# Decoder trunk on one core: the first norm's input read with channels on partitions

## What is computed

```
y = x * rsqrt(mean(x*x over channels) + 1e-6) * gain
layer 0:  x = x + dsa_attention(norm(x)) ;  x = x + swiglu(norm(x))
layer 1:  x = x + short_conv(norm(x))    ;  x = x + swiglu(norm(x))
```

## Time and profile before

| | us |
|---|---|
| median of 3 runs | 2071.18 |
| the profiled execution | 2071.52 |
| its span | 2069.9 |
| TensorE busy in the span | 2062.3 |
| VectorE busy | 1698.5 |
| ScalarE busy | 1177.7 |

### The profile page before, as it was taken

How to read it: one execution, slowest core, us unless ns; L and a number is a source line. 1 busy time by engine, 2 the same in 40 slices (tenths; PEclk the granted TensorE clock), 3 DMA queues, 4 the chain that set the end, 5 groups by cost and what they waited for, 6 DMA issues and landing times.

```text
span 2069.9 us, 27700 instructions
## 1 busy us (share of the span) xinstructions
PE 2062.3 (100%) x9421; PEld 1712.9 (83%) x9421; DVE 1698.5 (82%) x1933; ACT 1177.7 (57%) x1487; POOL 105.7 (5%) x128
## 2 busy tenths in 40 slices
PE   9999999999999999999999999999999999999999
PEld 8888888888888888888888888888888888888887
DVE  6777668999999987867798787579999999978766
ACT  6548656556655654545555554566656565654453
POOL 0000000100010000000000000000000000000000
PEclk9999999999999999999999999999999999999999
DMA  8564456777777776767666766567777777767674
GB/s 276 166 196 150 141 166 203 231 230 224 227 223 234 217 230 199 222 201 210 205 206 203 215 200 201 175 200 221 225 231 218 234 228 229 216 219 215 199 219 147
DMA packets 226722, 432.10 MB, mean 209 GB/s; under 512 B 14432, under 2 KB 21232, under 8 KB 226640
## 3 DMA queue, kind: packets, MB, share of 16 engines
q1 hardware_dynamic: 209328, 399.23, 58.8%
q0 software_dynamic: 17168, 31.75, 8.9%
q10 hardware_dynamic: 144, 0.03, 0.0%
HBM read 428.86 MB, written 2.10 MB: 208 GB/s over the span
## 4 chain that ended last, share of the span: by engine, by line
PE 97%; DVE 2%; ACT 1%; issue 1%; ACTq 0%; DVEq 0%
PE ps L733 24%; PE ps L735 24%; PE ps L734 24%; PE ps L589 3%; PE ps L522 3%; PE ps L524 3%; PE ps L523 3%; PE ps L590 3%; PE ps L591 3%; PE ps L538 2%; PE ps L695 1%; PE ps L693 1%; PE ps L694 1%; PE ps L648 1%; DVE w_lo L1356 0%
## 5 line engine op out<-in xcount | busy, mean ns | idle before, releaser
L1356 DVE TENSOR_TENSOR w_lo<-stage,w_hi 128x1024 fp32r<-128x1024 f32 x688 | 830.3, 1221 | 224.9 <-ACT w_hi L962 221.3
L962 ACT ACTIVATE w_hi<-stage 128x1024 fp32r<-128x1024 f32 x688 | 709.8, 1054 | 490.8 <-PE ps L735 365.6
L733 PE MATMUL ps<-w_hi,xs 128*128 128x512 f32 x1122 | 439.4, 392 | 0.3
L735 PE MATMUL ps<-w_hi,xs 128*128 128x512 f32 x1122 | 437.0, 389 | 0.0
L734 PE MATMUL ps<-w_lo,xs 128*128 128x512 f32 x1122 | 436.6, 389 | 0.0
L733 PEld LDWEIGHTS ps<-w_hi,xs 128*128 128x128 f32 x1122 | 210.7, 188 | 44.2 <-DVE gated L1637 1.1
L735 PEld LDWEIGHTS ps<-w_hi,xs 128*128 128x128 f32 x1122 | 210.6, 188 | 44.1
L734 PEld LDWEIGHTS ps<-w_lo,xs 128*128 128x128 f32 x1122 | 210.7, 188 | 42.9
L733 PE MATMUL ps<-w_hi,hs 128*128 128x512 f32 x584 | 227.6, 390 | 0.0
L735 PE MATMUL ps<-w_hi,hs 128*128 128x512 f32 x584 | 227.2, 389 | 0.0
L734 PE MATMUL ps<-w_lo,hs 128*128 128x512 f32 x584 | 227.2, 389 | 0.0
(11 more groups left out here) (217 smaller groups left out, 3041.2 us busy)
## 6 DMA issues: line engine op xcount, KB each, us to landing
stage<-in_w_gate SPq DMA_DIRECT2D x176, 512.0 KB, 4.0
stage<-in_w_up SPq DMA_DIRECT2D x176, 512.0 KB, 5.0
stage<-in_w_down SPq DMA_DIRECT2D x176, 512.0 KB, 5.0
stage<-in_conv_w_in SPq DMA_DIRECT2D x96, 512.0 KB, 4.9
stage<-in_attn_w_in SPq DMA_DIRECT2D x48, 512.0 KB, 4.4
stage<-in_w_gate POOLq DMA_DIRECT2D x86, 256.0 KB, 5.7
stage<-in_attn_w_out SPq DMA_DIRECT2D x32, 512.0 KB, 4.6
stage<-in_conv_w_out SPq DMA_DIRECT2D x32, 512.0 KB, 4.3
```

What stands on the lines that cost most here:

```text
L733: pe.matmul(ps[:, bank, :], hi, b_hi, start=start, stop=False)
L735: return pe.matmul(ps[:, bank, :], lo, b_hi, start=False, stop=stop)
L962: nc.scalar.activation(w_hi[:, j % RING, :], stage[:, at, :], ACT.Copy).then_inc(hi_done, 1)
L1356: tt(w_lo[:, p, :], stage[:, stage_at(first + j), :], f32(w_hi[:, p, :]), ALU.subtract).then_inc(lo_done, 1)
```

## The change

The host hands x over a second time, as `x_turned[p, k, t]` = x[token t, channel 128 k + p]. This is loaded into the same bytes of `res`, seen as 16 channel tiles of 256 tokens (`x_cols`). ScalarE and VectorE read it there instead of PSUM, and TensorE's transposes of x go. The identity is loaded after x and the first block. The rows are loaded into `res` during block 2, four loads. The squares are taken per channel tile; VectorE adds the 16 tiles to one, and TensorE sums over partitions by two matmuls with a column of ones. The steps that follow are put one to two slots later. TensorE issues 15 matmuls on the zeroed tile in one run.

```diff
-            sp.dma_start(mat.ap(), ident).then_inc(in_ident, 16)
-            load_x(x_part(0), in_x[0])
+            load_x(0, 2, in_x[0])
             load_front(0, 0)
-            load_x(x_part(1), in_x[1])
+            load_x(2, 4, in_x[1])
             load_front(0, 1)
             for j in range(1, 4):
-                load_x(slice(WIDE * j, WIDE * (j + 1)), in_x[j + 1])
+                load_x(4 * j, 4 * j + 4, in_x[j + 1])
                 load_front(0, 2 * j)
                 load_front(0, 2 * j + 1)
+            sp.dma_start(mat.ap(), ident).then_inc(in_ident, 16)
             for b in range(1, len(FRONT)):
                 for s in range(FRONT_SLOTS):
                     load_front(b, s)
+                    if b == 2 and s % 2:
+                        load_rows(s // 2)
...
+            def load_x(k0, k1, arrived):
+                sp.dma_start(x_cols[:, k0:k1, :], x_turned[:, k0:k1, :]).then_inc(arrived, 16)
+            def load_rows(j):
+                if j == 0:
+                    sp.wait_ge(res_squared, 4)
+                    sp.wait_ge(xs_ready, 4)
+                cols = slice(WIDE * j, WIDE * (j + 1))
+                sp.dma_start(res[:, :, cols], x[:, cols].rearrange("(a p) n -> p a n", p=P)).then_inc(in_rows, 16)
...
+            def sum_columns():
+                pe.wait_ge(squares_added, 5)
+                for a in range(2):
+                    mm = pe.matmul(ps[:, X_SUM_BANK, a:a + 1], square[:, 0, a * P:(a + 1) * P], ones[:, :],
+                                   start=True, stop=True)
+                mm.then_inc(first_summed, 1)
...
-            steps = {(1, 6): [lambda: index_turn(0)], (2, 0): [lambda: score_heads(0)],
+            steps = {(1, 2): [sum_columns], (1, 7): [lambda: index_turn(0)], (2, 1): [lambda: score_heads(0)],
...
-            warm(7)
-            pe.wait_ge(in_ident, 16)
-            turn_x(0)
-            warm(3)
-            turn_x(1)
-            warm(3)
+            warm(15)
             for b in range(len(FRONT)):
                 for s in range(FRONT_SLOTS):
                     front_slot(b, s)
-                    if b == 0 and s + 2 < 8:
-                        turn_x(s + 2)
...
-                    nc.scalar.activation(xs[:, k, 0:TOK], ps[:, X_BANKS[h % 4], TOK * m:TOK * (m + 1)],
+                    nc.scalar.activation(xs[:, k, 0:TOK], x_cols[:, k, :],
                                          ACT.Copy, scale=gain[:, 0, k:k + 1]).then_inc(res_hi, 1)
...
+            def x_square(j):
+                nc.scalar.activation(x_squares[j][:, :, :], x_cols[:, 4 * j:4 * j + 4, :],
+                                     ACT.Square).then_inc(res_squared, 1)
...
+            steps = {(1, 0): [lambda: x_square(0)], (1, 1): [lambda: x_square(1)],
+                     (1, 2): [lambda: x_square(2)], (1, 3): [lambda: x_square(3)],
+                     (1, 6): [first_root_step, lambda: evict(0), head_weights],
+                     (2, 3): [lambda: index_copy(0), lambda: evict(1)], (2, 5): [lambda: relu(0)],
...
+            def first_sum_a():
+                add_squares(square[:, :, :], cross[:, :, :], 0, 2)
+            def first_sum_b():
+                add_squares(sums[:, :, :], gated[:, :, :], 0, 4)
+            def first_sum_c():
+                add_squares(square[:, :, :], sums[:, :, :], 2, 4)
+                add_squares(square[:, 0:2, :], square[:, 2:4, :], 3, 4)
+                add_squares(square[:, 0, :], square[:, 1, :], 4, 4)
...
+            steps = {(1, 0): [set_score], (1, 2): [first_sum_a], (1, 3): [first_sum_b], (1, 4): [first_sum_c],
+                     (1, 6): [first_scale, lambda: rotate(0)],
+                     (2, 1): [head_tables], (2, 3): [lambda: rotate(1)], (2, 5): [lambda: add_scores(0)],
```

More of the change, by code:

```diff
@@ L80, in landed, with trunk @@
     return 16 * (n // DEEP + 1) + 16 * (loop_slots // DEEP) * i
-def trunk(nc, x, attn_w_in, attn_w_out, conv_w_in, conv_w_out, w_gate, w_up, w_down,
+def trunk(nc, x, x_turned, attn_w_in, attn_w_out, conv_w_in, conv_w_out, w_gate, w_up, w_down,
           gains, head_gains, conv_taps, tables_h, tables_i, ident, bounds, out):
@@ L127, in trunk @@
         rs = sb("rs", [P, 4, 2])
-        sb("to_64_bytes", [P, 10])
+        ones = sb("ones", [P, 1])
+        sb("to_64_bytes", [P, 9])
         part = ExitStack()
@@ L192, in trunk @@
         warm_rows = pt[:, 0:P]
+        x_cols = res[:, :, :].rearrange("p a (k t) -> p (a k) t", t=TOK)
+        x_squares = (square, cross, sums, gated)
         swapped, roped, squared = (by_rows(buf) for buf in (cross, sums, square))
@@ L233, in trunk @@
         rs_ready = sem("rs_ready")
-        x_turned = sem("x_turned")
+        in_rows = sem("in_rows")
+        squares_added = sem("squares_added")
         x_low = sem("x_low")
@@ L324, in merged @@
             return out
-        X_BANKS = (2, 3, 6, 7)
+        X_SUM_BANK = 4
         FRONT_BANKS = ((0, 1), (2, 3))
@@ L331, in trunk @@
         INDEX_HEADS = tuple(tuple(12 + h if i == 0 else 4 * (i - 1) + h for h in range(4)) for i in range(4))
-        def x_part(h):
-            return slice(2 * P * h, 2 * P * (h + 1))
         def x_low_done(engine, h):
@@ L432, in load_block @@
                     load(n + s, s % DEEP, w[s * 2 * P:(s + 1) * 2 * P, base:][:, bass.ds(col, width)], width)
-            def load_x(cols, arrived):
-                sp.dma_start(res[:, :, cols], x[:, cols].rearrange("(a p) n -> p a n", p=P)).then_inc(arrived, 16)
+            def load_x(k0, k1, arrived):
[6 more added lines that the diff above has]
+                sp.dma_start(res[:, :, cols], x[:, cols].rearrange("(a p) n -> p a n", p=P)).then_inc(in_rows, 16)
             def load_front(b, s):
@@ L529, in stream_rows @@
                         other()
-            pe.wait_ge(warm_set, 1)
+            pe.wait_ge(warm_set, 2)
             def turn_rows(rows, bank):
@@ L596, in index_turn @@
                 if b == 0:
+                    pe.wait_ge(in_ident, 16)
                     pe.wait_ge(index_added, 1)
@@ L972, in res_high @@
             def res_high(q, j, bank=TURN_BANK):
-                act.wait_ge(res_turned, 4 * q + j + 1)
+                act.wait_ge(res_turned, 4 * (q - 1) + j + 1)
                 for m in range(4):
@@ L1020, in x_high @@
             def x_high(h):
[L1022 to L1025, removed]
+                if h < 3 or h % 2 == 0:
+                    act.wait_ge(in_x[h if h < 2 else h // 2 + 1], 16)
                 for m in range(2):
                     k = 2 * h + m
-                    nc.scalar.activation(xs[:, k, 0:TOK], ps[:, X_BANKS[h % 4], TOK * m:TOK * (m + 1)],
+                    nc.scalar.activation(xs[:, k, 0:TOK], x_cols[:, k, :],
                                          ACT.Copy, scale=gain[:, 0, k:k + 1]).then_inc(res_hi, 1)
[L1031 to L1037, removed]
+            def x_square(j):
+                nc.scalar.activation(x_squares[j][:, :, :], x_cols[:, 4 * j:4 * j + 4, :],
+                                     ACT.Square).then_inc(res_squared, 1)
             def first_root_step():
@@ L1042, in first_root_step @@
                 act.wait_ge(const_set, 2)
-                nc.scalar.activation(root[:, 0, :], ssum[:, 0, :], ACT.Sqrt, bias=eps[:, 0:1],
+                nc.scalar.activation(root[:, 0, :], ps[:, X_SUM_BANK, 0:2], ACT.Sqrt, bias=eps[:, 0:1],
                                      scale=1.0 / D).then_inc(first_root, 1)
@@ L1136, in out_high @@
                                          ps[:, 4 + a, :].rearrange("p (h q) -> p h q", h=4), ACT.Copy).then_inc(o_hi, 1)
+            act.dma_start(gain.ap(), gains).then_inc(in_gain, 16)
             act.preload_act_table(ACT.Sqrt)
-            act.dma_start(gain.ap(), gains).then_inc(in_gain, 16)
             act.wait_ge(in_gain, 16)
[L1141 to L1144, removed]
+            steps = {(1, 0): [lambda: x_square(0)], (1, 1): [lambda: x_square(1)],
+                     (1, 2): [lambda: x_square(2)], (1, 3): [lambda: x_square(3)],
+                     (1, 6): [first_root_step, lambda: evict(0), head_weights],
+                     (2, 3): [lambda: index_copy(0), lambda: evict(1)], (2, 5): [lambda: relu(0)],
                      (2, 7): [lambda: index_copy(1)], (3, 1): [lambda: relu(1)], (3, 3): [lambda: evict(2)],
@@ L1371, in x_low_step @@
             def x_low_step(h):
+                if h < 3 or h % 2 == 0:
+                    dve.wait_ge(in_x[h if h < 2 else h // 2 + 1], 16)
                 dve.wait_ge(res_hi, 2 * h + 2)
@@ L1376, in x_low_step, with add_squares @@
                     ins = nc.vector.scalar_tensor_tensor(
-                        xs[:, k, TOK:], ps[:, X_BANKS[h % 4], TOK * m:TOK * (m + 1)], gain[:, 0, k:k + 1],
+                        xs[:, k, TOK:], x_cols[:, k, :], gain[:, 0, k:k + 1],
                         f32(xs[:, k, 0:TOK]), ALU.mult, ALU.subtract)
                 ins.then_inc(xs_ready if h % 2 else x_low, 1)
-            def first_sum():
-                dve.wait_ge(res_squared, 4)
```

(18 more changed lines are left out.)

## The result

The changed kernel takes 2093.32 us (median of 4 runs, 2093.04 to 2094.12) against 2071.23 us for the kernel before beside it: ratio 1.0107, 95% interval 1.0095 to 1.0119. It is 22 us slower where 3.6 us faster was forecast.

A forecast was written before the change was run, and what follows sets the result against it. TensorE's work list plus its start bounds the kernel; block 0 ends 5.2 us earlier, less a 1.2 us wait and 0.45 us for two column matmuls: 3.6 us gain, 2071.18 - 3.6 = 2067.6 us, range 2065.4 to 2069.6.

The forecast's parts named there:

- The step that failed: Rule for TensorE's list behind the start of (1,3): the end moves as much as that start, 3.6 us earlier.
- (1,3): Fourth slot of block 1, behind all new TensorE work; its start was forecast at 31.1 us instead of 34.73.
- Memset, `gain`'s earlier load: free: Small additions of the change, the memset and an earlier load of gain, taken to cost nothing.
- if records behind it are spaced wider than 0.173 us: Sign of failure: TensorE's matmul records behind its one gap, after slot (1,2), stand further apart than 0.173 us.
- four rivals: No wait at sum, 2066.4 (0.12); clock falls, 2070.4 (0.07); loads bind, 2068.1 (inside forecast's 0.76); turned x slow, 2073.1 (0.05).
- Rival 2: TensorE's clock falls to half pace in the 1.2 us wait: 2.8 us lost, gain 0.8, 2070.4 us; chance 0.07.
- stop of TensorE, by the starts: TensorE's wait behind slot (1,2) for VectorE's last addition, from 29.5 to 30.65 us: 1.2 us.
- the upper bound (0.7): Block 0's loads: longer runs of x might bring data another 0.7 us earlier; lower bound nothing.
- the 0.5 us that I gave it: SyncE's queue beginning with x instead of the identity: all that follows lands 0.5 us earlier.
- The sum late next: Sum of squares behind slot (1,2) waits for VectorE's additions, done at 30.5 us; TensorE stops 1.2 us.
- x from SBUF: ScalarE's 16 high parts cost 0.05 us more each from SBUF than from PSUM; VectorE's taken as no change.
- Rows, identity, warm matmuls, later steps: Row loads, identity's landing, the warm run of 15 and steps behind (1,3) cost nothing; closest cover there 2 us.

The follow-up runs named there:

- e1_aligned: The changed kernel with its last pad cut from 36 to 32 bytes, so hs and sx begin at byte 139136 again: 2067.13 us, ratio 0.9981.
- e7: e1_aligned with the identity's load first in SyncE's queue again, ahead of x: 2067.84 us, ratio 0.9983.
- e8: e1_aligned without the four loads of x's rows and the wait for them, so without the input's residual: 2067.11 us, ratio 0.9981.
- e4_xs_shift32: The kernel before with 32-byte pads ahead of and behind xs, so xs moves 32 bytes and later tiles 64: 2121.14 us, ratio 1.0240.
- e5_w_shift32: The kernel before with 32-byte pads ahead of w_hi and behind w_lo, so these move 32 bytes and later tiles 64: 2118.65 us, ratio 1.0228.
- e10_all_shift32: The kernel before with one 32-byte pad ahead of w_hi, moving all operands by 32 bytes with their distances kept: 2071.16 us, ratio 0.9999.

## Why the prediction was wrong

The step that failed stands in its first paragraph: "If the list behind some point is unchanged and the other engines keep ahead of it, the end moves by as much as TensorE moves there." The list was unchanged (the first `index_turn` and `score_heads` stand one slot later) and the others kept ahead, but the instructions in it had got new addresses, and with them a new length: 26.4 us behind (1,3), a term that the sum does not have. With the old addresses (e1_aligned) the step holds to 0.03 us. Where the term belonged, the prediction has "Memset, `gain`'s earlier load: free": I did not ask where the tile that the memset writes pushes the others. No rival had it, and the mark for failure that comes closest ("if records behind it are spaced wider than 0.173 us") does not catch it as it stands, since it was set for matmuls of 384 columns, and these keep their pace: the two slots from (1,4) on take 4.16 us in both kernels. None of the four rivals happened. Rival 2 comes nearest, longer matmuls, but the granted clock stays at 1.00, and it is the matmuls of 512 columns with displaced operands that grow.

The steps of the front, forecast against the changed kernel:

| | forecast | measured |
|---|---|---|
| weights landed: second, third, last slot | 8.1, 10.4, 17.7 | 7.3, 9.7, 16.8 |
| third slot starts | 12.15 | 11.58 |
| block 1 starts | 23.3 | 22.73 |
| last addition done | 30.5 | 29.7 |
| stop of TensorE, by the starts | 1.2 | 0.8 |
| two matmuls of one column | 0.45 | 0.47 |
| (1,3) starts | 31.1 | 30.25 |

The landings are from issue and duration; those of the third and of the last slot's weights:

```profile
stage<-in_attn_w_in SPq DMA_DIRECT2D x1, 336.0 KB, 6.4
...
stage<-in_attn_w_in SPq DMA_DIRECT2D x1, 336.0 KB, 9.4
```

issued at 3.28 and 7.42 us. They came 0.7 to 0.9 us earlier than I took, about the upper bound (0.7) that I had put on the longer runs of x; the first stretch moved 344 GB/s against 300. In e7 the identity's place makes no clear difference by the third slot, so the 0.5 us that I gave it may have had the wrong cause; the early landings are then left to the longer runs (argued, not tried by itself).

**The sum late next**: right. VectorE's chain of additions in the changed kernel, which ends the wait:

```profile
23.17 1.22 DVE L1383 TENSOR_TENSOR square<-square,cross 128x1024 f32<-128x1024 f32 x1
24.31 0.95 DVE L1364 TENSOR_TENSOR w_lo<-stage,w_hi 128x768 fp32r<-128x768 f32 x1
25.18 1.22 DVE L1383 TENSOR_TENSOR sums<-sums,gated 128x1024 f32<-128x1024 f32 x1
26.31 0.95 DVE L1364 TENSOR_TENSOR w_lo<-stage,w_hi 128x768 fp32r<-128x768 f32 x1
27.18 1.22 DVE L1383 TENSOR_TENSOR square<-square,sums 128x1024 f32<-128x1024 f32 x1
28.50 1.22 DVE L1383 TENSOR_TENSOR square<-square 128x512 f32<-128x512 f32 x2
```

Each has the length that the forecast gave it (1.22, 1.14 back to back, 0.87 for a split, 1.2 for the last two with a handover), the chain only begins 0.9 us earlier. It is VectorE's own work, as forecast.

**x from SBUF**: two high parts take 0.89 to 0.91 us, 0.84 from PSUM before: 0.03 us more each, against 0.05 forecast. VectorE's low parts stayed at 0.88 for two. The Trainium skill ("VectorE: DVE Perf Modes", the errata section) has VectorE cheaper from SBUF than from PSUM; this trace shows no difference.

**Rows, identity, warm matmuls, later steps**: no gap of TensorE opens between (1,3) and 62 us, e8 prices the rows at nothing, and with the place mended the end moves by 4.2 us where the front moved by 4.3. For the front the forecast was 0.7 us short by e1_aligned, 0.9 by the changed kernel; e1_aligned's 2067.13 lies within 0.5 us of the forecast 2067.6.

## What to carry to other kernels

A new tile is never free until the addresses behind it have been compared: a tile of 4 bytes (per partition) moved `hs` and `sx`, 88 KB of a partition, by 32 bytes and cost 26 us, six times what the change won. Where a kernel is bound by TensorE with matmuls like these, of 512 columns, keep the moving and the stationary operands at the same place modulo 256 bytes of a partition, and look at the start-to-start time of matmuls in lines that a change does not touch before looking for its waits. And put a wait where the data have had time to come: one slot later in TensorE's list gave 1 us.

## What was not expected of the hardware

- A float32 matmul of this kernel, with a stationary operand of 128x128 and 512 moving columns, steps at 226.8 to 227.0 ns when the distance between its operands' addresses is a multiple of 256 bytes, and at 232.5 to 233.3 ns at distances of 16, 32, 64 and 128 bytes (the table). It does not matter which operand is displaced (e4_xs_shift32, e5_w_shift32), nor does it if both are displaced together by 32 bytes (e10_all_shift32).
- Matmuls of 384 and 336 columns pay little or nothing: with `xs` or the weights displaced by 32 bytes their median steps are 173 to 174 and 153 to 154 ns, 173 and 154 in the kernel before; only with `xs` displaced by 16 bytes do those of 384 columns rise, to 176. Why 512 columns differ is open, as is the mechanism.
- Neighbours matter too. Products of `xs` at distance 0 rise to 227.4 and 227.5 where `sx` and `hs` are displaced, and those of `t_hi` with `sx` at distance 0 in e4_xs_shift32 to 394 and 396 ns a record, beside displaced products of `xs`. In most steps both matmuls use the same stationary tile, so the runs do not tell whether the distance counts within one matmul or between its moving operand and the next one's stationary operand. The few mixed steps fit neither alone. In the changed kernel a step from `t_hi` with `sx` (32) to `t_hi` with `xs` (0) takes 235.8 ns, although `t_hi` is at distance 0 from the next stationary operand; one from `w_hi` with `xs` (0) to `w_hi` with `sx` (32) takes 236.6 ns, although the matmul that it leaves is at distance 0.
- ScalarE's and VectorE's instructions on the displaced weights keep their lengths within 3 ns: the high part of 1024 columns takes 1.054 us in the kernel before and 1.057 in e5_w_shift32, the low part 1.221 in both.
